# Modulation weights as k-tiles in 8 KB runs, a new order of the first loads, and the context norm between projections

## The chip, the cores and the metric

The kernel runs on one core of a Trainium2 chip. The metric is the device time of one execution in microseconds (us), the median of three runs. The core has five engines that run their own instruction streams and wait for each other on semaphores: TensorE (PE in the profile), VectorE (DVE), ScalarE (ACT), GpSimd (POOL) and SyncE (SP). DMAs are issued by SP, ACT or POOL and carried out by 16 DMA engines.

## The reference, cut to what matters

The reference computes a transformer block with attention and a mixture of experts, and then two more layers of dense mixers. The change lies wholly in the first block, up to its residual sum:

```
mod_l = (silu(c) @ w_ada + b_ada).reshape(6, d)            # c: the condition, d = 1024
mod_c = (silu(c_ctx) @ w_ada + b_ada).reshape(6, d)
sh1, sc1, gt1, sh2, sc2, gt2 = mod_l
hl = rms_norm(x, g_mix) * (1 + sc1) + sh1                  # x: 256 tokens x 1024
pl = hl @ w_in                                             # 1024 x 2048: q, k, v, f
q, k = rope(pl q part), rope(pl k part)
hc = rms_norm(ctx, g_mix) * (1 + csc1) + csh1              # ctx: 256 x 1024
kc, vc = hc @ w_in[:, k and v part]
mix = [diff_attention(q, [kc, k], [vc, v]), fourier_mix(f)]
x = x + gt1 * (mix @ w_out)
h2 = rms_norm(x, g_ffn) * (1 + sc2) + sh2                  # then the experts
```

`w_ada` is 1024 x 6144 in fp32 (24 MB). Its first 2048 columns give sh1 and sc1, which the first projection needs; the other 4096 give gt1, sh2, sc2 and gt2, which are needed only after attention.

## The kernel before

**Tiling.** Weights come in units of 1 MB through a ring of four slots (`ring`). `U_ADA1` are 8 units for sh1 and sc1, `U_IN` 8 units of `w_in`, `U_ADA2` 16 units for the rest of the modulation, `U_OUT` 4 units of `w_out`; then come the experts. A unit of `w_ada`, `w_in` or `w_out` holds all 1024 rows of 256 columns, so its DMA moves 1 KB runs. The experts' units are cut so that a run is 8 KB.

**Order of the loads.** SP issues the units in the order of their numbers. Before each it waits (`vacant`, L532) until the unit four back has been used: `unit_done` for a modulation unit, `w_lo_ready` for a projection's. ACT issues all the rest at its start (L1327 to L1334): the constants' first part, 17 short rows of parameters (among them c, c_ctx and the table of relative positions), x, ctx, the constants' second part, and five side tensors.

**Modulation.** silu(c) and silu(c_ctx) are two columns of a 32 wide stationary tile `csil`. `ada_rows` (L744) takes two units into one PSUM bank of `acc`; four groups of 32 partitions each sum a quarter of the k-tiles. ACT copies the bank out (`mod_row`, L1347), and `ada_cols` (L756) sums the four groups against a selector `sel` and turns the row into columns, four small matmuls for 512 columns. DVE adds the bias (L1844) and makes the scale `a_mix`.

**Before the first projection.** PE waits for the parameter rows, transposes them, takes two pairs of modulation units, transposes x and ctx (L772, L780), and runs the other pairs with the two norms' sums (L722) between them. DVE then scales x by the norm and by 1 + sc1 (L1862), ACT adds the shift and rounds to the high part `h_hi` (L1385), and DVE makes the low part `h_lo` (L1867).

**The projections.** Each fp32 weight unit is split too, by ACT (`split_high`, L497) and DVE (`split_low`, L506), and `project3` runs three matmuls (L669 to L671) in place of an fp32 one. Units 2 to 5 of `w_in` are also used for ctx in plain fp32 (L704, L712). ACT copies each bank out (L1449).

**Attention.** Eight steps s of 128 queries: PE's scores of step s + 1 (L881), then `ada_cols` of the pair before (L761), `ada_rows` of pair 4 + s (L751), the transposes of step s (L890), and after every second step the product with the values (L900). DVE takes maxima (L1895) and combines (L1902 to L1905), ACT exponentiates (L1484). In step 7 ACT has, in this order: the high part of `w_out` unit 0 (`split_high(8)`, issued at the end of step 6), the last `mod_row`, the high part of unit 1 (`split_high(9)`), and the copy of the step's transposes (L1493), for which the last `values` waits.

## Time and profile before

| | us |
|---|---|
| median of 3 runs | 1971.18 |
| lowest and highest | 1965.08 and 1974.21 |
| the profiled execution's own time | 1973.52 |
| its span in the trace | 1971.7 |

The trace's times count from the span's start; some 1.8 us of the profiled execution lie outside the span. The page gives each engine's busy time and the chain of work that ended last. For this change the averages over the span say little: the timelines of the first 215 us, one per engine, say which wait ends last in each stage.

### The profile page before, as it was taken

To read this page: it belongs to the slowest core of one execution; us is meant where nothing else is said; L and a number is where in the kernel's file an instruction comes from. 1 tells how busy PE (TensorE), PEld (TensorE's weight loads), DVE (VectorE), ACT (ScalarE), POOL (GpSimd) and SP (SyncE) were. 2 spreads that over 40 slices of the span, in tenths; PEclk is the share of its full clock that TensorE was granted. 3 is DMA by queue.
4 is the path that set the end of the run, shared out by engine and by line. 5 is a ranking of instruction groups with operands and counts; after the bars stand their busy time and mean duration, and the time that the engine had idled before them with its cause. 6 is when DMAs were issued, how large, how long until landed. Compare 5 with 4: busy or idle time off the path is not lost.

```text
span 1971.7 us, 31086 instructions
## 1 busy us (share of the span) xinstructions
PE 1859.7 (94%) x13331; PEld 1559.5 (79%) x13331; DVE 826.6 (42%) x982; ACT 660.6 (34%) x773; POOL 160.9 (8%) x75
## 2 busy tenths in 40 slices
PE   4898869999999997999999999999999999899998
PEld 2895754445545546999998999999998899899998
DVE  0523531111111117544676554465545345565444
ACT  2514320000000005434435544354344445354433
POOL 0000000000000000111000021112111000111110
PEclk9899969999999998999999999999999999999999
DMA  9336659999999995555534255555554445345550
GB/s 288 123 107 215 216 212 422 421 421 421 422 422 422 422 419 186 180 183 187 177 129 150 98 181 191 174 189 183 182 187 134 150 150 171 129 150 194 192 173 40
DMA packets 224062, 444.26 MB, mean 225 GB/s; under 512 B 11130, under 2 KB 183891, under 8 KB 199259
## 3 DMA queue, kind: packets, MB, share of 16 engines
q1 hardware_dynamic: 217888, 435.74, 60.2%
q10 hardware_dynamic: 6076, 7.08, 1.1%
q8 instruction: 77, 1.26, 0.3%
q14 instruction: 21, 0.17, 0.0%
HBM read 441.73 MB, written 1.06 MB: 225 GB/s over the span
## 4 chain that ended last, share of the span: by engine, by line
PE 88%; DVE 5%; ACT 3%; issue 1%; ACTq 1%; DMA 1%; POOL 0%; DVEq 0%
PE wk L669 13%; PE wk L670 13%; PE wk L671 13%; PE wk L1013 11%; PE acc L669 6%; PE wk L1033 6%; PE acc L671 6%; PE acc L670 6%; PE wk L977 3%; PE acc L993 3%; ACT w_hi L497 1%; PE acc L751 1%; DVE w_lo L506 1%; ACTq L1334 1%; DVE con L2069 1%
## 5 line engine op out<-in xcount | busy, mean ns | idle before, releaser
L506 DVE TENSOR_TENSOR w_lo<-ring,w_hi 128x2048 fp32r<-128x2048 f32 x198 | 452.3, 2287 | 438.4 <-ACT w_hi L497 438.3
L497 ACT ACTIVATE w_hi<-ring 128x2048 fp32r<-128x2048 f32 x199 | 379.4, 1908 | 477.0 <-PE wk L671 319.8
L669 PE MATMUL wk<-h_hi,w_hi 128*128 128x256 f32 x1832 | 524.9, 286 | 14.9 <-DVE h_lo L2058 10.2
L670 PE MATMUL wk<-h_lo,w_hi 128*128 128x256 f32 x1832 | 522.2, 285 | 0.0
L671 PE MATMUL wk<-h_hi,w_lo 128*128 128x256 f32 x1832 | 522.1, 285 | 0.0
L669 PEld LDWEIGHTS wk<-h_hi,w_hi 128*128 128x128 f32 x1832 | 354.7, 194 | 17.9 <-issue 14.4
L670 PEld LDWEIGHTS wk<-h_lo,w_hi 128*128 128x128 f32 x1832 | 354.6, 194 | 0.2
L671 PEld LDWEIGHTS wk<-h_hi,w_lo 128*128 128x128 f32 x1832 | 354.4, 193 | 0.0
L669 PE MATMUL acc<-hid_hi,w_hi 128*128 128x256 f32 x896 | 255.2, 285 | 3.4 <-POOL hid_lo L1766 3.4
L671 PE MATMUL acc<-hid_hi,w_lo 128*128 128x256 f32 x896 | 254.3, 284 | 0.0
L670 PE MATMUL acc<-hid_lo,w_hi 128*128 128x256 f32 x896 | 254.2, 284 | 0.0
L1766 POOL TENSOR_TENSOR hid_lo<-gated,hid_hi 128x512 fp32r<-128x512 f32 x44 | 125.3, 2848 | 1185.8 <-ACT hid_hi L1605 1185.8
L669 PEld LDWEIGHTS acc<-hid_hi,w_hi 128*128 128x128 f32 x896 | 172.2, 192 | 3.6 <-issue 3.6
L670 PEld LDWEIGHTS acc<-hid_lo,w_hi 128*128 128x128 f32 x896 | 172.2, 192 | 0.0
L671 PEld LDWEIGHTS acc<-hid_hi,w_lo 128*128 128x128 f32 x896 | 172.1, 192 | 0.0
L1013 PE MATMUL wk<-ring,arena 128*64 128x512 f32 x512 | 112.6, 592 | 0.8 <-ACT arena L1555 0.8
L1013 PE MATMUL wk<-ex_ring,arena 128*64 128x512 f32 x512 | 112.6, 592 | 0.0
L1555 ACT ACTIVATE arena<-wk 128x512 f32<-128x512 f32 x32 | 19.1, 597 | 267.5 <-PE wk L977 267.5
L669 PE MATMUL wk<-w_hi,h_hi 128*128 128x256 f32 (+1 forms) x336 | 99.9, 297 | 2.9 <-DVE h_lo L2058 2.9
L2022 DVE SCALAR_TENSOR_TENSOR arena<-wk,slot_gate,arena 128x512 f32<-128x512 f32 x16 | 12.0, 751 | 209.2 <-PE wk L1013 209.2
L670 PE MATMUL wk<-w_lo,h_hi 128*128 128x256 f32 (+1 forms) x336 | 96.0, 286 | 0.0
L671 PE MATMUL wk<-w_hi,h_lo 128*128 128x256 f32 (+1 forms) x336 | 96.0, 286 | 0.0
(299 smaller groups left out, 1991.5 us busy)
## 6 DMA issues: line engine op xcount, KB each, us to landing
ring<-in_ffn_w_in_dram SPq DMA_DIRECT2D x88, 1024.0 KB, 5.0
ring<-in_w_gate_dram SPq DMA_DIRECT2D x64, 1024.0 KB, 13.8
ex_ring<-in_w_up_dram SPq DMA_DIRECT2D x64, 1024.0 KB, 17.1
ring<-in_ffn_w_out_dram SPq DMA_DIRECT2D x44, 1024.0 KB, 4.8
ex_ring<-in_w_down_dram SPq DMA_DIRECT2D x32, 1024.0 KB, 13.6
arena<-in_w_down_dram SPq DMA_DIRECT2D x32, 1024.0 KB, 12.7
ring<-in_w_ada_dram SPq DMA_DIRECT2D x24, 1024.0 KB, 8.8
ring<-in_b_w_in_dram SPq DMA_DIRECT2D x24, 1024.0 KB, 5.2
```

What stands on the lines that cost most here:

```text
L497: nc.scalar.activation(w_hi[:, v % SPLIT, 0:n], ring[:, u % RING, 0:n], ACT.Copy).then_inc(w_hi_ready, 1)
L506: eng.tensor_tensor(w_lo[:, v % SPLIT, 0:n], ring[:, u % RING, 0:n], w_hi[:, v % SPLIT, 0:n].bitcast(F32), ALU.subtract).then_inc(w_lo_rea ...
L669: mm(dst, w[0], x[0], start=first, stop=False, skip_group_check=True)
L670: mm(dst, w[0], x[1], start=False, stop=False, skip_group_check=True)
L671: return mm(dst, w[1], x[0], start=False, stop=last, skip_group_check=True)
L751: last = mm(accf[lane:lane + 32, bank * 512 + j * UW:bank * 512 + (j + 1) * UW], csil[:, k, :], slot_cols(u)[:, k, :], start=(k < ADA_GROU ...
L977: last = mm(wk[:, 1, q * P:(q + 1) * P], h2[:, t, 4 * half + q, :], pick_at[:, t, :], start=(t == 0), stop=(t == TT - 1))
L993: last = mm(acc[:, m, :], y_rows[:, m * P:(m + 1) * P], spread[:, p % 2, :], start=(p == 0 and m % 2 == 0), stop=True, skip_group_check=True)
L1013: last = mm(wk[own, s // 2, :], xg[:, p % 2, k, own], ex_slot(2 * s + j)[:, q * DE:(q + 1) * DE], start=(k == 0), stop=(k == KT - 1), skip ...
L1033: last = mm(wk[own, 2 + half, :], hidT[:, 2 * s + f, own], ex_slot(8 + 2 * s + j)[:, c:c + 512], start=(s == 0 and f == 0), stop=(s == 1 a ...
L1334: act.dma_start(dst, src).then_inc(side_in, 16)
L1766: nc.gpsimd.tensor_tensor(dst, src, hi.bitcast(F32), ALU.subtract).then_inc(ready, 1)
```

## The change

- **Loads of the modulation.** `ada_v` is cut by k-tile: a unit is 128 rows of 2048 columns, so a run is 8 KB, and eight units make one group of 2048 columns. Units stay 1 MB, and there are still 8 and 16.
- **Modulation on PE.** A unit is four matmuls with 512 columns instead of eight with 256; they accumulate over eight units in one bank. Each of the four partition groups now holds other columns, so `sel` gets 8 columns and `ada_cols` runs once for 2048 columns, with the same four matmuls: three times in all instead of twelve.
- **Order of the loads.** x goes first on SP's queue, then the eight units, two units of `w_in`, ctx, and the rest. On ACT's queue c and c_ctx come right after the constants' first part, which shrinks (642 to 264 columns). The second part and the side tensors (cut in two where they are the router's) are issued by POOL after the first projection's unit is done.
- **Order on PE.** c is transposed first, then x, then the modulation units in the order of arrival with the parameter rows' transposes and x's norm among them. The first projection unit starts in halves. The transposes of ctx come after it, the norm of ctx and the matmul for lambda after the second unit, the table of relative positions after the fourth. The ctx projections of units 2 and 3 come after both units' three-piece ones.
- **x's chain.** DVE multiplies x by the inverse root (one instruction) before the modulation is there. Then ACT makes `h_hi` with scale and shift in one step, and DVE the unrounded value (`shifted`) and the low part.
- **Attention.** The transposes of all steps use one PSUM bank, `ada_cols` runs before step 4's units and at the end.

```diff
+            sp.dma_start(x_rows, x[0].rearrange("(t p) d -> p t d", p=P)).then_inc(x_in, 16)
             for a in range(8):
-                fetch(U_ADA1 + a, slot_cols(U_ADA1 + a), ada_v[a])
-            for a in range(8):
+                fetch(U_ADA1 + a, ring[:, (U_ADA1 + a) % RING, :], ada_v[0, a])
+            for a in range(2):
+                fetch(U_IN + a, slot_cols(U_IN + a), in_v[a])
+            sp.dma_start(c_rows, ctx[0].rearrange("(t p) d -> p t d", p=P)).then_inc(ctx_in, 16)
+            for a in range(2, 8):
                 fetch(U_IN + a, slot_cols(U_IN + a), in_v[a])
...
+            def ada_rows(u, k, bank):
+
+                arrived(u)
+                for gr in range(ADA_GROUPS):
+                    last = mm(accf[32 * gr:32 * gr + 32, bank * 512:(bank + 1) * 512], csil[:, k, :],
+                              ring[:, u % RING, gr * 512:(gr + 1) * 512], start=(k == 0), stop=(k == KT - 1),
+                              skip_group_check=True)
+                last.then_inc(unit_done, 1)
...
+            def first_unit(b):
+
+                pe.wait_ge(first_lo, 1)
+                project3(b, 0, fresh=0, ks=range(KT // 2), closes=False)
+                split(U_IN)
+                return project3(b, 0, fresh=0, ks=range(KT // 2, KT), opens=False)
+
+            pe.wait_ge(std_ready, 1)
+            group(first_unit, ends_unit=True)
+            pe.wait_ge(ctx_in, 16)
+            pe.wait_ge(mod_ready, 1)
+            for t in range(TT):
+                for k in range(KT):
+                    last = nc.tensor.transpose(acc[:, k, t * P:(t + 1) * P], c_rows[:, t, k * P:(k + 1) * P], ident)
+            last.then_inc(ctx_ps, 1)
+            v = split(U_IN + 1)
+            group(lambda b: project3(b, v), ends_unit=True)
+            norm(1, 0, accf[:, 0:T])
...
+            for a in range(2, 4):
                 v = split(U_IN + a)
-                group(lambda b: project3(b, v, fresh=None if a else 0), ends_unit=True)
-            pe.wait_ge(lame_ready, 1)
+                group(lambda b: project3(b, v))
+            pe.wait_ge(tables_in, 16)
+            mm(accf[0:HEADS2, 512:1024], reltab[:, :], buckets[0:32, :], start=True, stop=True).then_inc(rel_ps, 1)
+            pe.wait_ge(h_shifted, 1)
...
-                if s:
-                    ada_cols(3 + s)
-                    pe.wait_ge(at_ready, s)
-                ada_rows(4 + s, (s + 1) % 2)
+                if s == 4:
+                    ada_cols(1)
+                for a in (2 * s, 2 * s + 1):
+                    ada_rows(U_ADA2 + a, a % KT, 1)
                 turn(s)
...
-            act.dma_start(con[:, FIRST:], consts[:, FIRST:]).then_inc(tables_in, 16)
-            for dst, src in SIDE:
-                act.dma_start(dst, src).then_inc(side_in, 16)
...
+            def scaled_high(k):
+
+                A(h_hi[:, k, :], hT[:, k, :], ACT.Identity, bias=mod[:, k, 0:1],
+                  scale=a_mix[:, 0, k:k + 1]).then_inc(h_hi_ready, 1)
...
+            pool.wait_ge(unit_done, U_IN + 1)
+            pool.dma_start(con[:, FIRST:], consts[:, FIRST:]).then_inc(tables_in, 16)
+            for dst, src in SIDE:
+                pool.dma_start(dst, src).then_inc(side_in, 16)
...
+            def shifted(k):
+
+                return V.tensor_scalar(hcT[:, k, :], hT[:, k, :], a_mix[:, 0, k:k + 1], mod[:, k, 0:1], ALU.mult, ALU.add)
```

PE, from its start to the first projection, before (L740 to L743 the parameter rows, L751 modulation, L772 x, L780 ctx, L761 the turn into columns, L722 the norms):

```order
L740 MATMUL wk<-con,scr 128x128
L741 MATMUL wk<-con,scr 128x89
L742 MATMUL wk<-con,scr 64x4
L743 MATMUL wk<-con,reltab 8x512
L751 MATMUL acc<-ring,gated 32x256 x32
L772 MATMUL acc<-con,arena 128x128 x16
L780 MATMUL wk<-con,arena 128x128 x16
L751 MATMUL acc<-ring,gated 32x256 x16
L761 MATMUL acc<-con,gated 128x2 x8
L722 MATMUL wk<-scr,con 128x256 x8
L751 MATMUL acc<-ring,gated 32x256 x16
L722 MATMUL wk<-scr,con 128x256 x8
```

The same stretch of PE now (L770 is c, L774 x, L754 modulation, L780 to L782 the parameter rows, L734 x's norm, L764 the columns, L680 the first projection):

```order
L770 MATMUL acc<-con,scr 128x16
L774 MATMUL wk<-con,arena 128x128 x16
L754 MATMUL acc<-ring,gated 32x512 x8
L780 MATMUL acc<-con,scr 128x128
L781 MATMUL acc<-con,scr 128x73
L782 MATMUL acc<-con,scr 64x4
L754 MATMUL acc<-ring,gated 32x512 x8
L734 MATMUL wk<-scr,con 128x256 x8
L754 MATMUL acc<-ring,gated 32x512 x16
L764 MATMUL acc<-con,gated 128x8 x4
L680 MATMUL wk<-h_hi,w_hi 128x256
```

What is gone from this stretch is the table of relative positions, the transposes of ctx, one norm and three of four turns into columns; a modulation matmul is twice as wide and there are half as many.

ACT before, its last DMA issues and what follows:

```order
L1329 DMA scr<-in_rel_table_dram 32x8
L1330 DMA arena<-in_x_dram 128x2x1024
L1331 DMA arena<-in_ctx_dram 128x2x1024
L1332 DMA con<-in_consts_dram 128x2888
L1334 DMA arena<-in_w_fourier_dram 128x4x128
L1334 DMA arena<-in_w_router_group_dram 128x8x4
L1334 DMA arena<-in_w_router_expert_dram 128x8x32
L1334 DMA arena<-in_b_router_group_dram 1x4
L1334 DMA arena<-in_b_router_expert_dram 1x32
L1337 ACT_TABLE_LOAD
L1337 ACTIVATE cols<-wk 128x128
```

ACT now, from the same place (L1347 is the silu, L1349 to L1351 the parameter columns, L1363 x's squares, L1358 the copy of the modulation rows):

```order
L1344 DMA reltab<-in_rel_table_dram 32x8
L1347 ACT_TABLE_LOAD
L1347 ACTIVATE gated<-acc 128x8x2
L1349 ACTIVATE cols<-acc 128x128
L1350 ACTIVATE cols<-acc 128x73
L1351 ACTIVATE cols<-acc 64x4
L1363 ACTIVATE scr<-xT 128x512 x4
L1369 ACT_TABLE_LOAD
L1369 ACTIVATE std<-wk,small 128x256
L1358 ACTIVATE gated<-acc 128x512
```

Eight issues are gone from between the parameter rows and ACT's first activation.

PE in attention, steps 1 and 2 before (L881 scores, L761 columns, L751 modulation, L890 transposes):

```order
L881 MATMUL wk<-arena 128x512 x2
L761 MATMUL acc<-con,gated 128x2 x4
L751 MATMUL acc<-ring,gated 32x256 x16
L890 MATMUL acc<-con,arena 128x128 x4
L881 MATMUL wk<-arena 128x512 x2
L761 MATMUL acc<-con,gated 128x2 x4
L751 MATMUL acc<-ring,gated 32x256 x16
L890 MATMUL acc<-con,arena 128x128 x4
```

and now:

```order
L894 MATMUL wk<-arena 128x512 x2
L754 MATMUL acc<-ring,gated 32x512 x8
L903 MATMUL acc<-con,arena 128x128 x4
L894 MATMUL wk<-arena 128x512 x2
L754 MATMUL acc<-ring,gated 32x512 x8
L903 MATMUL acc<-con,arena 128x128 x4
```

The turn into columns is gone from between the scores and the modulation units.

## Rows read from the trace of the kernel before

**Rows 1.** The page, busy time of each engine and its share of the span.
```profile
PE 1859.7 (94%) x13331; PEld 1559.5 (79%) x13331; DVE 826.6 (42%) x982; ACT 660.6 (34%) x773; POOL 160.9 (8%) x75
```
**Rows 2.** Windows by stage: length, busy time per engine, PE's clock, DMA share, GB/s.
```profile
0.00:63.20 63.20, 27.46 (x231) 18.65 (x231) 12.81 (x24) 20.89 (x33) 0.20 (x4) 0.97 0.89 285
63.20:139.60 76.40, 76.35 (x511) 73.05 (x512) 22.93 (x24) 22.30 (x28) 3.13 (x2) 0.96 0.31 98
160.70:214.00 53.30, 43.95 (x405) 26.38 (x403) 25.76 (x53) 26.10 (x55) 0.36 (x1) 0.92 0.97 309
```
**Rows 3.** Timeline of 0:32: start us, us, engine, line, instruction.
```profile
7.57 0.32 ACTq L1329 DMA_DIRECT2D reltab<-in_rel_table_dram  x1
11.41 10.72 ACTq L1334 DMA_DIRECT2D arena<-in_w_router_expert_dram  x1
12.64 0.45 PE L740 MATMUL wk<-con,scr 128*128 128x128 f32 x1 [12.64 <-DMA reltab<-in_rel_table_dram]
26.32 1.28 ACT L1337 ACT_TABLE_LOAD   x1 [26.32 <-issue]
30.12 6.20 PE L751 MATMUL acc<-ring,gated 128*32 128x256 f32 x64 [14.94 <-ACT gated L1343]
```
**Rows 4.** Pieces of the chain that ended last, 30:64: start us, us, what.
```profile
37.13 1.95 PE acc L772 x16
...
43.39 1.88 PE acc L761 x16
...
50.69 3.67 PE wk L722 x16
...
58.98 0.18 DVE small L1844 x2
...
59.46 3.26 DVE scr L1862 x8
62.71 0.41 DVE h_lo L1867
...
63.25 0.55 PE wk L669
```
**Rows 5.** Windows, columns as in rows 2: 1 KB runs from SP, then the experts' 8 KB.
```profile
0.00:10.00 10.00, 0.00 (x0) 0.00 (x0) 0.37 (x3) 0.00 (x0) 0.20 (x4) 1.00 0.86 244
...
180.00:200.00 20.00, 18.59 (x192) 11.36 (x184) 9.77 (x24) 10.16 (x24) 0.00 (x0) 1.00 1.09 349
...
400.00:700.00 300.00, 300.00 (x1574) 147.56 (x1572) 37.37 (x121) 23.88 (x40) 0.00 (x0) 1.00 1.01 422
```
**Rows 6.** Timeline: single instructions that price an operation of the change.
```profile
13.31 1.87 PE L743 MATMUL wk<-con,reltab 32*8 32x512 f32 x2
...
163.29 0.49 DVE L1904 TENSOR_SCALAR arena<-arena,small 128x512 f32<-128x512 f32 x1
...
228.48 1.22 DVE L1926 TENSOR_TENSOR h_lo<-arena,h_hi 128x1024 fp32r<-128x1024 f32 x1 [1.13 <-ACT h_hi L1531]
```
**Rows 7.** Windows, columns as in rows 2: the first 6 us of the projections.
```profile
63.20:69.40 6.20, 6.15 (x29) 6.18 (x30) 6.20 (x16) 4.68 (x11) 0.00 (x0) 0.50 0.05 18
```
**Rows 8.** Timeline of attention, 160:218: DVE's end of two steps, PE, then ACT.
```profile
176.32 0.75 DVE L1905 SCALAR_TENSOR_TENSOR arena<-arena,small 128x512 f32<-128x512 f32 x1
...
181.14 0.75 DVE L1905 SCALAR_TENSOR_TENSOR arena<-arena,small 128x512 f32<-128x512 f32 x1
...
167.34 1.86 PE L761 MATMUL acc<-con,gated 128*128 128x2 f32 x8
...
205.07 1.07 PE L751 MATMUL acc<-ring,gated 128*32 128x256 f32 x16 [1.84 <-DMA ring<-in_w_ada_dram]
...
213.96 3.75 PE L900 MATMUL acc<-arena 128*128 128x256 f32 x8 [2.33 <-ACT arena L1499]
...
208.12 1.91 ACT L497 ACTIVATE w_hi<-ring 128x2048 fp32r<-128x2048 f32 x1 [6.19 <-DMA ring<-in_w_out_dram]
...
211.14 1.91 ACT L497 ACTIVATE w_hi<-ring 128x2048 fp32r<-128x2048 f32 x1 [0.63 <-DMA ring<-in_w_out_dram]
```

285 lines of the change are left out of this document (146 added, 139 removed).

## The prediction

> **What bounds the kernel now.** I read the page first. PE is busy for 94% of the span [rows 1], which looks as if loads at the start could not matter. But the average covers stages with different limits, and the change touches only the first 214 us. The windows by stage [rows 2] divide them: up to 63.2 us PE works 27.46 us of 63.20; from there to 139.6 it works without a gap (76.35 of 76.40); in attention, 160.7 to 214.0, the DMAs are busy for 0.97 of the time. So the start and attention can give something, and in the projections every microsecond of PE work added is a microsecond lost.
>
> In the start, the timeline shows two waits. PE could begin at 12.64 us, when the last parameter row has landed, but ACT is still issuing DMAs: one of the router's takes 10.72 us of its queue, and ACT's first activation starts at 26.32. Since silu(c) comes after it, the first modulation matmul starts at 30.12 [rows 3], when four units have long been in the ring and no further one could be fetched. From there to 63.25 the chain is PE work of x, ctx, two norms and the modulation, then DVE and ACT [rows 4].
>
> In attention the chain passes through DMAs. ACT's high part of the first `w_out` unit waits 6.19 us for its DMA until 208.12, that of the second until 211.14, and behind both stands the copy for which the last product with the values (213.96) waits [rows 8]. At 1 KB runs the queue moves 349 GB/s; in the experts, at 8 KB, it moves 422 [rows 5].
>
> **The start.** With ACT's queue ending at the parameter rows (7.57 + 0.32), the silu is ready near 9.5 us, and x, now first on SP's queue, near 6. From then on the modulation is bound by its DMAs: each slot is freed by a unit's matmuls, some 1.6 us [rows 3], less than a unit's transfer. What must have landed is x and eight units, 9.4 MB, and 0.2 MB of small things. I take for the first 10 us what it moved before, 244 GB/s or 2.4 MB, and for the other 7.2 MB the 422 GB/s of 8 KB runs [rows 5]: 17.0 us. The last unit is there at 27.0. At the 349 GB/s of 1 KB runs it would be 30.6; these are the two ends of this term, and I take the first because the row with the same run length and the same SP queue is the nearest.
>
> Behind it lies a chain: the last unit's matmuls 1.7 us (64 records, four units' worth, took 6.20, a part of it at the lower clock; so 1.55 for one unit, and a little more if all of it is at the lower clock) [rows 3]; ACT's copy 0.6; four small matmuls 1.0 at the upper clock (16 records took 1.88 [rows 4]) and 1.9 at the lower [rows 8], I take 1.4; the bias and scale on DVE 0.5 to 1.2 (58.98 to 59.46, and what lies before), I take 1.0. That makes 31.7. DVE then computes eight unrounded tiles. The tensor-scalar of 512 columns took 0.49 [rows 6]; with some 0.2 of it fixed, one of 256 costs 0.27 in a row, 2.2 in all; the upper bound is the 3.26 of L1862 [rows 4]. A half of `w_lo` is 1.22 [rows 6], the first `h_lo` 0.41 [rows 4], hand-overs 0.4: the first three-piece matmul starts at 36.0, in place of 63.25. ACT's `h_hi` and the first `w_in` unit (3.0 us behind the last modulation unit, 30.0, and its half high part 31.0) come earlier than that and cost nothing; if that cover goes, a late `w_in` unit costs its lateness. **Term: -27.2 us**, with ends of -30 (short DVE steps, PE at full clock) and -22.5 (1 KB rate and the slow DVE row).
>
> **The projections.** Their own work stays, 76.4 us, with the same slow beginning at half clock [rows 7]. What moves in between them is on PE, with nothing to hide it: ctx's transposes 1.9 (16 records, as x's in 1.95), one norm 1.9 (half of 3.67) [rows 4], the sum for lambda 0.3, and the table of relative positions 1.2 to 1.9 (1.87 at 13.31 [rows 6]). **Term: +5.4 us.** Waits that could be added: ctx has landed by 38, before the first unit ends (44). The second norm's squares end near 50.5, while PE is in unit 2 until 51.6. The matmul of relative positions waits for POOL's DMA of 1.7 MB, issued at 44 and wanted at 65; behind that wait PE's remaining projections are queued. `h_shifted` is there near 60. I cost these at nothing, by 1 to 20 us of cover.
>
> Here the Trainium skill speaks against the change: its page "SBUF — State Buffer", § SBUF: two separate sides, says that a DMA issued by POOL gets its descriptors from GpSimd, which cannot write them while VectorE holds the shared port. No run here shows a DMA from POOL. By that rule the tables would come late by part of DVE's busy time in that stretch; the cover of 21 us would have to be used up before it costs.
>
> **Attention.** Ten modulation units are moved in the saturated part, now in 1.049 MB / 422 GB/s = 2.49 us instead of 3.00: 5.1 us. It also begins earlier: the columns' 1.86 us before step 1's units, at the lower clock [rows 8], are gone. That gives 1.9 us more for the first `w_out` unit, 201 instead of 208.1. But then the steps themselves are as long: one without a DMA wait takes 181.14 - 176.32 = 4.82 us from combine to combine, where two units take 4.98, and three of the eight also hold a product with the values, at full clock half of 3.75 [rows 8]. This chain ends within 2 us of the DMA. **Term: -7.0 us**, ends -2 (units no faster, only the start earlier) and -8.5 (the 1.84 us wait at 205.07 gone as well).
>
> **What follows.** The experts' loads wait for free slots, not for a time, so that nothing there absorbs the shift: their stage is bound at 422 GB/s [rows 5] from when it begins, and it begins later than its slots are filled. The code from there is the same.
>
> **Sum.** 1973.5 of the profiled execution - 27.2 + 5.4 - 7.0 = 1944.7. That execution is 2.3 us over the median, so against the median 1942.4; I say 1942.
>
> **Rivals.**
> 1. *8 KB runs of w_ada move no faster than 1 KB runs.* For it: rows of `w_ada` lie 24 KB apart, while an expert's tile is read in one piece, so the 422 may belong to the layout. Against it: 349 is also the rate of every 1 KB load I looked at. Then the start gives 23.6 instead of 27.2 and attention 2 to 3: 1942 + 3.6 + 4.5 = 1950, with a late `w_in` 1952. The skill's page "DMA: Bandwidth & Descriptors", § Where 436 GB/s comes from, would have it so: it says that for loads from HBM the memory side, about 358 GB/s for a core, is the limit. By that rule, the trace disagrees: 422 over 300 us. Chance 0.12.
> 2. *A hand-over comes late.* The short rows (512 B) share the DMA engines with packets of 4 and 8 KB. If the parameter rows land not at 12.6 but at 22, PE's wait for them stands in front of the third unit, no slot is freed, and the queue runs dry for some 5 us. The same price has a stall of ctx's squares or of the tables. 1947 to 1952. Chance 0.13.
> 3. *More is gained*: the start at 33 and attention -8.5, 1936. Chance 0.08.
> 4. *The gain is given back*: some wait later is tied to the DMAs' progress and not to PE's. I found none; 1966 to 1976. Chance 0.03.
> 5. *Slower.* The tables and side tensors through POOL. PE's queue stands behind the tables' landing in the middle of the projections. It costs only when they land after 65 us, and turns the gain of 29 into a loss when they land after 94, 50 us from their issue. The nearest row is ACT's 10.72 us for one router tensor [rows 3]; at that price for each of eight transfers, and with the tables served last, they land at 44 + 86 = 130, 65 us late, and the kernel takes 1942 + 65 = 2007. It needs that order or that price for the tables alone; issued first, they are more likely near one such price, 55 us, inside the cover. Chance 0.02.
>
> **How the numbers follow.** The forecast has 0.62, its own range 1937 to 1947. The range that should hold the time 8 times in 10 leaves out rivals 4 and 5 and about half of what is over 1950 and under 1936: 1934 to 1953. A measurement of this kernel tells 0.5%, some 10 us, from no change; so all under 1961 is faster: 0.62 + 0.12 + 0.13 + 0.08 = 0.95, and I give 0.94. Same 0.04, slower 0.02.
>
> **What would show it.** Right: ACT's first activation before 10 us; the eight modulation units' matmuls one every 2.5 us, the last near 27; the first three-piece matmul at 34 to 38; PE without gaps until about 117; over 400 GB/s in attention; the `w_out` wait ending near 179 (201 - 22). Wrong: modulation matmuls 3 us apart (rival 1), a gap of PE before the parameter rows' transposes or before ctx's norm (rival 2), PE waiting for a DMA issued by POOL (rival 5), or an end of the first block that moves less than the first projection does.

## The result, and the profile after

The changed kernel takes **1945.72 us** (median of four runs, 1943.99 to 1947.01), beside 1972.36 for the kernel before, measured with it: ratio 0.9872, 95% interval 0.9849 to 0.9895. It is 26.6 us faster; forecast were 29, with the time at 1942. In the measurements of the experiments the kernel before had medians of 1969.5 to 1970.5, so the difference is good to some 2 us. The profiled execution took 1944.74 us, its span is 1943.0.

Windows by stage (length, busy time per engine in the order PE, PEld, DVE, ACT, POOL, then PE's clock, DMA share, GB/s), to set against [rows 2, 5]:

```profile
0.00:10.00 10.00, 2.75 (x13) 2.75 (x14) 0.36 (x3) 1.47 (x2) 0.20 (x4) 1.00 0.81 301
10.00:20.00 10.00, 5.06 (x33) 1.79 (x35) 2.58 (x4) 0.95 (x5) 0.00 (x0) 0.94 1.02 416
20.00:30.00 10.00, 9.45 (x64) 3.99 (x52) 3.31 (x2) 3.32 (x6) 0.00 (x0) 0.89 0.85 292
30.00:37.20 7.20, 1.50 (x14) 0.97 (x8) 5.58 (x16) 3.82 (x7) 0.00 (x0) 0.67 1.08 378
37.20:120.20 83.00, 82.95 (x548) 77.96 (x549) 24.77 (x26) 31.75 (x43) 8.57 (x10) 0.97 0.45 153
141.20:189.30 48.10, 35.21 (x229) 15.74 (x227) 25.94 (x55) 22.73 (x49) 0.33 (x1) 0.97 0.95 348
```

The start is 26 us shorter. The projections are still all PE (82.95 of 83.00) but take 83.0 us where they took 76.5. In the start the rate is 416 GB/s while modulation units come in. In attention it is 348 on average: 415 at 150 to 160, less where the DMAs have nothing to fetch, and the `w_out` units at its end move in 1 KB runs.

The start on PE (timeline: start us, us, engine, line, instruction; the bracket is idle time ahead and what ended it), to set against [rows 3, 4]. L770 is c, L774 x, L754 modulation, L780 the parameter rows, L734 x's norm, L764 the columns, L680 the first three-piece matmul:

```profile
7.25 0.26 PE L770 MATMUL acc<-con,scr 16*128 16x16 f32 x1 [7.25 <-DMA scr<-in_c_ctx_dram]
7.43 3.67 PE L774 MATMUL wk<-con,arena 128*128 128x128 f32 x16
11.04 2.49 PE L754 MATMUL acc<-ring,gated 128*32 128x512 f32 x16
18.47 0.33 PE L780 MATMUL acc<-con,scr 128*128 128x128 f32 x1 [4.94 <-DMA reltab<-in_rel_table_dram]
...
22.39 3.72 PE L734 MATMUL wk<-scr,con 128*128 128x256 f32 x16
26.05 2.78 PE L754 MATMUL acc<-ring,gated 128*32 128x512 f32 x24
29.37 1.06 PE L754 MATMUL acc<-ring,gated 128*32 128x512 f32 x8 [0.55 <-DMA ring<-in_w_ada_dram]
31.16 1.06 PE L764 MATMUL acc<-con,gated 128*128 128x8 f32 x8 [0.72 <-ACT gated L1358]
37.25 0.55 PE L680 MATMUL wk<-h_hi,w_hi 128*128 128x256 f32 x1 [5.04 <-DVE h_lo L1892]
```

The first modulation matmul comes at 11.04 in place of 30.12, the first three-piece one at 37.25 in place of 63.25. One wait stands where the forecast had none: 4.94 us for the parameter rows, whose last landed at 18.47, 10.9 us after its issue at 7.57. While PE stood there no slot was freed, and the 292 GB/s at 20 to 30 us show the hole that this left (391 in the same ten microseconds of the kernel with late rows, below).

What was put between the projections, from the chain of work that ended last (start us, us, what): ctx's transposes, its norm, lambda, the table of relative positions.

```profile
45.63 1.75 PE acc L814 x16
...
53.13 3.45 PE acc L734 x16
56.58 0.31 PE acc L820 x2
...
68.60 0.95 PE acc L825 x2
```

POOL's DMA issues in the same stretch; no instruction of PE waits for what they load. The constants' second part landed 9.5 us after its issue, and PE wanted it at 68.5:

```profile
45.95 0.73 POOL L1797 DMA_DIRECT2D con<-in_consts_dram  x1 [45.42 <-PE wk L682]
46.67 0.80 POOL L1799 DMA_DIRECT2D arena<-in_w_fourier_dram  x1
56.59 0.77 POOL L1799 DMA_DIRECT2D arena<-in_w_router_group_dram  x1 [9.12 <-issue]
```

The end of attention, to set against [rows 8], PE and then ACT. L903 are the transposes of the last step, L913 products with the values, L504 high parts of `w_out`, L1504 the copy of the transposes:

```profile
179.92 0.66 PE L903 MATMUL acc<-con,arena 128*128 128x128 f32 x4
180.41 1.89 PE L913 MATMUL acc<-arena 128*128 128x256 f32 x8
185.92 1.77 PE L764 MATMUL acc<-con,gated 128*128 128x8 f32 x8 [2.76 <-ACT gated L1358]
189.30 3.73 PE L913 MATMUL acc<-arena 128*128 128x256 f32 x8 [1.60 <-ACT arena L1510]
...
183.47 1.91 ACT L504 ACTIVATE w_hi<-ring 128x2048 fp32r<-128x2048 f32 x1 [4.71 <-DMA ring<-in_w_out_dram]
185.29 0.58 ACT L1358 ACTIVATE gated<-acc 128x512 f32<-128x512 f32 x1
186.49 1.91 ACT L504 ACTIVATE w_hi<-ring 128x2048 fp32r<-128x2048 f32 x1 [0.62 <-DMA ring<-in_w_out_dram]
188.30 0.58 ACT L1504 ACTIVATE arena<-acc 128x512 f32<-128x512 f32 x1
```

The wait for `w_out` ends last again. All times that the experiments are compared by, from PE's timelines (us; the rope matmuls end the projections; "values" is the last product with the values, "router" the router's first matmul):

| kernel | first three-piece | to rope | first scores | to values | router | time |
|---|---|---|---|---|---|---|
| before | 63.25 | 76.5 | 158.78 | 55.2 | 254.1 | 1972.4 |
| changed | 37.25 | 83.0 | 139.25 | 50.1 | 228.6 | 1945.7 |
| short runs | 40.49 | 82.6 | 142.07 | 51.9 | 236.9 | 1952.2 |
| rows late | 35.06 | 82.8 | 136.88 | 48.2 | 225.1 | 1943.9 |
| tables on ACT | 48.30 | 82.1 | 149.44 | 50.1 | 239.8 | 1955.6 (one run) |
| side tensors by POOL, in before | 57.33 | 76.1 | 152.47 | 52.0 | 247.5 | 1963.3 |
| quarter units | 36.82 | 83.2 | 139.01 | 48.6 | 231.2 | 1948.1 (one run) |
| columns each step | 37.84 | 82.0 | 138.91 | 49.5 | 227.4 | 1948.4 (one run) |
| tail order | 37.88 | 81.9 | 138.77 | 44.6 | 229.3 | 1947.5 |
| tail order, filler | 38.04 | 82.2 | 139.22 | 44.6 | 228.0 | 1947.7 |
| rows late, filler | 35.36 | 80.9 | 135.29 | 50.0 | 224.9 | 1943.1 |
| ctx early | 38.44 | 75.4 | 132.84 | 50.3 | 222.6 | 1941.1 |
| ctx early, halves | 37.64 | 76.7 | 133.33 | 50.0 | 222.6 | 1941.3 |
| ctx early, split norm | 40.51 | 77.9 | 137.42 | 50.8 | 228.0 | 1942.8 |

The quarter units leave out three quarters of the later modulation, so only the stretch up to the router is read there. The intervals of the ratios to the kernel before are given where one decides.

### The profile page after: what moved, and what is told of

It reads as the page before. It is cut to its first block, busy times and chain, and to the rows that moved or that the text cites. A ratio compares the mean times of both kernels' runs of the same rounds, so it can differ in the third digit from the quotient of the medians.

```text
span 1943.0 us, 30548 instructions
## 1 busy us (share of the span) xinstructions
PE 1845.9 (95%) x13068; PEld 1542.4 (79%) x13068; DVE 828.1 (43%) x986; ACT 655.1 (34%) x767; POOL 166.9 (9%) x83
## 3 DMA queue, kind: packets, MB, share of 16 engines
HBM read 441.73 MB, written 1.06 MB: 228 GB/s over the span
## 4 chain that ended last, share of the span: by engine, by line
PE 88%; DVE 6%; ACT 3%; DMA 1%; issue 1%; ACTq 0%; POOL 0%; DVEq 0%
PE wk L680 13%; PE wk L681 13%; PE wk L682 13%; PE wk L1026 11%; PE wk L1046 6%; PE acc L680 6%; PE acc L682 6%; PE acc L681 6%; PE wk L990 3%; PE acc L1006 3%; ACT w_hi L504 1%; DVE con L2112 1%; DVE w_lo L513 1%; PE wk L1258 1%; PE wk L715 1%
## 5 line engine op out<-in xcount | busy, mean ns | idle before, releaser
L680 PE MATMUL wk<-h_hi,w_hi 128*128 128x256 f32 x1832 | 526.3, 287 | 14.5 <-DVE h_lo L2101 9.5
L504 ACT ACTIVATE w_hi<-ring 128x2048 fp32r<-128x2048 f32 x198 | 377.4, 1907 | 481.0 <-PE wk L682 324.7
L680 PEld LDWEIGHTS wk<-h_hi,w_hi 128*128 128x128 f32 x1832 | 357.2, 195 | 17.5 <-issue 14.7
L680 PE MATMUL acc<-hid_hi,w_hi 128*128 128x256 f32 x896 | 254.5, 284 | 3.2 <-POOL hid_lo L1779 3.2
L680 PEld LDWEIGHTS acc<-hid_hi,w_hi 128*128 128x128 f32 x896 | 171.9, 192 | 3.3 <-issue 3.3
L680 PE MATMUL wk<-w_hi,h_hi 128*128 128x256 f32 (+1 forms) x336 | 98.4, 293 | 3.0 <-DVE h_lo L2101 3.0
L1026 PEld LDWEIGHTS wk<-ring,arena 128*64 128x64 f32 x512 | 37.1, 137 | 73.0 <-issue 72.2
```

Source lines behind the costliest of these rows:

```text
L504: nc.scalar.activation(w_hi[:, v % SPLIT, 0:n], ring[:, u % RING, 0:n], ACT.Copy).then_inc(w_hi_ready, 1)
L680: mm(dst, w[0], x[0], start=first, stop=False, skip_group_check=True)
L1026: last = mm(wk[own, s // 2, :], xg[:, p % 2, k, own], ex_slot(2 * s + j)[:, q * DE:(q + 1) * DE], start=(k == 0), stop=(k == KT - 1), skip ...
```

## The experiments

**Run length.** Each modulation unit of the changed kernel as two DMAs of 1 KB runs:

```diff
+                dst = ring[:, u % RING, :].rearrange("p (i j f) -> p j i f", j=2, f=UW)
+                src = src.rearrange("p (i j f) -> p j i f", j=2, f=UW)
+                sp.dma_start(dst[:, 0], src[:, 0]).then_inc(odd_in[u % RING], 16)
+                sp.dma_start(dst[:, 1], src[:, 1]).then_inc(weights_in[u % RING], 16)
...
-                fetch(U_ADA1 + a, ring[:, (U_ADA1 + a) % RING, :], ada_v[0, a])
+                fetch_short(U_ADA1 + a, ada_v[0, a])
```

> The kernel after, with every modulation unit moved in 1 KB runs: two DMAs for a unit, one for the even and one for the odd 256-column pieces; bytes, order and everything else as after. Theory (the run length sets the rate): about 350 GB/s in attention in place of over 400, the last modulation unit of the start 1 to 3 us later, the first three-piece matmul at 38 to 41 in place of 37.25, and from the first scores to the last product with the values 53 to 55 us in place of 50.05; in all 5 to 9 us slower than after. Rival (the rate belongs to something else, the layout or the queue): both as after within 1 us. The same run tells why the parameter rows land at 18.5: if they share the DMA engines packet by packet with 4 and 8 KB packets, they land by 14 here; if it is the number of bytes ahead of them, they stay at 18 or later.

1952.22, ratio 0.9911 (0.9887 to 0.9934), +6.5 us. PE's timeline of that kernel (here L764 is modulation, L790 the rows), and its window of 10 to 20 us:

```profile
14.03 0.33 PE L790 MATMUL acc<-con,scr 128*128 128x128 f32 x1
...
16.03 1.06 PE L764 MATMUL acc<-ring,gated 128*32 128x512 f32 x8 [1.48 <-DMA ring<-in_w_ada_dram]
19.06 1.93 PE L764 MATMUL acc<-ring,gated 128*32 128x512 f32 x8 [1.96 <-DMA ring<-in_w_ada_dram]
```
```profile
10.00:20.00 10.00, 5.37 (x39) 1.43 (x38) 2.58 (x4) 3.80 (x8) 0.00 (x0) 0.88 1.10 347
```

A unit every 3.03 us, 347 GB/s for 416. The edit also makes two DMAs of each unit, but the kernel before moved 1 KB runs in one DMA per unit at 349 GB/s [rows 5], so it is the run length that sets the rate, and the prediction's first rival is out. Of the 8.3 us at the router, run length explains 2.8 (first scores) and 1.9 (attention); the other 3.7 come behind attention, mostly from a collision of DVE and POOL that is shown with the tail's experiments. And PE does not wait for the rows, which have landed by 14.03 instead of 18.47: short rows on ACT's queue are held up by long runs on SP's. That agrees with the Trainium skill, "DMA: Bandwidth & Descriptors", § Queues, rings and completion order, which says that a DMA engine serves its queues in turn and drains a whole packet of several descriptors from one before it switches.

**Rows late.** The parameter rows get a place of their own, and PE takes them after x's norm:

```diff
-            pe.wait_ge(rows_in, 16 * N_ROWS)
-            nc.tensor.transpose(accf[:, 16:16 + P], rows1, ident)
...
             for a in range(2, 4):
                 ada_rows(U_ADA1 + a, a, 3)
             pe.wait_ge(x_ready, 1)
             norm(0, 0)
+            pe.wait_ge(rows_in, 16 * N_ROWS)
+            nc.tensor.transpose(accf[:, 16:16 + P], rows1, ident)
...
```

ACT's copies of these rows and what DVE computes from them move behind the norm too, so ACT's squares of x no longer stand behind the wait.

> The kernel after, with the parameter rows in a place of their own and their transposes and copies moved behind x's norm, so that PE doesn't wait for them before the third modulation unit. Theory (the late rows hold back the slots, and so the loads): the third unit's matmuls start near 14 in place of 18.94, the last unit lands near 27 in place of 29.4, the first three-piece matmul starts near 35 in place of 37.25; 2 us off the time. Rival (the loads are bound by bytes and start-up alone, PE's wait is hidden): the last unit still lands at 29 or later and nothing is gained.

The last modulation unit comes at 27.16, a unit every 2.5 us, and the first three-piece matmul at 35.06, 2.2 us earlier; the whole 1943.87 (ratio 0.9879, 0.9856 to 0.9902), and the router 3.5 us earlier. The theory holds in the trace; in the medians the difference to the changed kernel, 1.9 us, is inside their spread.

**ACT's queue.** The tables and side tensors of the changed kernel back on ACT, behind the rows; and, the other way round, the side tensors of the kernel before issued by POOL:

```diff
+            act.dma_start(con[:, FIRST:], consts[:, FIRST:]).then_inc(tables_in, 16)
+            for dst, src in SIDE:
+                act.dma_start(dst, src).then_inc(side_in, 16)
...
-            pool.wait_ge(unit_done, U_IN + 1)
-            pool.dma_start(con[:, FIRST:], consts[:, FIRST:]).then_inc(tables_in, 16)
-            for dst, src in SIDE:
-                pool.dma_start(dst, src).then_inc(side_in, 16)
```

> The kernel after, with one part undone: the constants' second part and the side tensors (the router's still cut in two) are issued by ACT behind the parameter rows, as before, not by POOL. Theory (ACT's queue blocks): ACT's first activation at 20 to 27 in place of 9.27, the first three-piece matmul at 48 to 54. Rival (cut in two they don't block the queue; only their 1.9 MB share the DMAs): first activation by 12, first three-piece matmul at 40 to 43.

> The kernel before, with one part of the change alone: the side tensors (router and Fourier weights, router biases) are issued by POOL after the first projection unit, not by ACT before its first activation. Theory (most of the start's gain is that ACT's queue no longer blocks the silu): the first modulation matmul at 17 to 18 in place of 30.12, the first three-piece matmul near 51 in place of 63.25, nothing else moves; 12 us faster than before. Rival (the loads bind the start anyway): the first three-piece matmul at 56 or later.

ACT's timeline with the tables on ACT:

```profile
8.55 8.08 ACTq L1347 DMA_DIRECT2D arena<-in_w_router_group_dram  x2
16.65 4.30 ACTq L1347 DMA_DIRECT2D arena<-in_w_router_expert_dram  x2
...
21.88 1.28 ACT L1350 ACT_TABLE_LOAD   x1 [21.88 <-issue]
```

Halved, the router's tensors still take 12.4 us of the queue; the first three-piece matmul comes 11 us later, as the theory has it, and the whole is at 1955.6. In the kernel before, freeing the queue moves the first modulation matmul from 30.12 to 18.15 and the first three-piece one by only 5.9 us (1963.26, ratio 0.9971, 0.9957 to 0.9984), since then PE waits for units; that is the rival's case, not the theory's:

```profile
18.15 4.36 PE L753 MATMUL acc<-ring,gated 128*32 128x256 f32 x48 [2.54 <-ACT gated L1342]
26.25 1.93 PE L753 MATMUL acc<-ring,gated 128*32 128x256 f32 x16 [3.74 <-DMA ring<-in_w_ada_dram]
```

So in the kernel before the queue alone is worth 6 of the start's 26 us, and in the changed one, where the loads come faster, 11; the rest needs the order of the loads, the run length and the shorter chain with it.

**Attention: what bounds it now.** Two changes to the changed kernel, one that takes load off the DMAs and one that puts the columns back:

```diff
-                fetch(U_ADA2 + a, ring[:, (U_ADA2 + a) % RING, :], ada_v[1 + a // KT, a % KT])
+                fetch(U_ADA2 + a, ring[:, (U_ADA2 + a) % RING, 0:512], ada_v[1 + a // KT, a % KT][:, 0:512])
```
```diff
                 if s == 4:
                     ada_cols(1)
+                elif s:
+                    for m in range(4):
+                        mm(accf[:, 1216 + 8 * m:1224 + 8 * m], ones, sel, start=True, stop=True)
```

> The changed kernel, in which each of the sixteen later modulation units loads only the first 512 of its 2048 columns, 2 KB runs and a quarter of the bytes. The rest of the slot keeps what was there, so three quarters of gt1, sh2, sc2 and gt2 are left out and the routing after attention may differ: only the stretch before the router is read. In the changed kernel the first scores start at 139.25, the last product with the values at 189.30, 50.05 us later. Theory A (the eight steps are bound by the chain PE, DVE, ACT, 4.82 us a step, and only the tail behind the last step by the loads of w_out): the steps stay at 4.82, the last combine stays 39.0 us behind the first scores, the first w_out unit no longer keeps ACT waiting, its high part starts near 178.8 and the last product with the values near 184.7, 45.4 us behind the first scores. Theory B (the loads bind the steps too): the steps fall under 4.82 and the last product comes at 178 or earlier, under 39 us. Theory C (the tail is not bound by loads either): 189, 50 us.

> The changed kernel with four more small matmuls between scores and modulation units in steps 1 to 3 and 5 to 7, where the kernel before turned its pair of units into columns; their result is not used. What the removed turns into columns were worth in attention: theory A (PE is idle 1.25 us in each step, waiting for DVE's combine, so 1.06 us of small matmuls fit in): the steps stay at 4.82 us, the slots come free about 1 us later, and the last product with the values starts 0 to 1.2 us later, 50.1 to 51.3 us behind the first scores. Theory B (they lengthen the steps): six times 1.06, 56.4 us.

In the changed kernel DVE's combines stand 4.81, 4.83, 4.82, 6.55, 4.83, 6.55 us apart (6.55 where a product with the values lies between). With a quarter of the bytes they stand as far apart, but for one step in which PE's clock was low (0.81 at 141 to 150): the steps are not bound by loads. The tail is only in part: ACT still waits for `w_out`, until 181.75,

```profile
181.75 1.91 ACT L504 ACTIVATE w_hi<-ring 128x2048 fp32r<-128x2048 f32 x1 [2.04 <-DMA ring<-in_w_out_dram]
```

5.4 us after the issue at 176.37, in place of 8.05 after 175.42. The load is issued when step 6 frees a slot, so it comes at the steps' pace, not at the DMAs'. Theory A had the mechanism right and expected 3.2 us too much of it (48.6 us to the values, not 45.4), 1.2 of which are the slow step. With the columns back attention is no longer (49.5), Theory A: in the steps without a product PE idles 1.25 us, which is room for 1.06 us of small matmuls. (The router comes at 231.2 in the first of these, later than in the changed kernel; the next section tells why.)

A slow step is also in the profiled execution of the kernel before, and a larger one. Its step 1 took 7.7 us. The kernel before with the side tensors by POOL runs the same instructions in attention, and its step 1 took 4.8. The windows of that step, first the kernel before, then the other:

```profile
164.60:172.30 7.70, 7.68 (x48) 4.06 (x48) 2.86 (x6) 2.13 (x6) 0.00 (x0) 0.56 0.66 217
```
```profile
158.30:163.10 4.80, 4.56 (x48) 2.62 (x48) 2.85 (x6) 2.25 (x7) 0.00 (x0) 1.00 1.00 331
```

PE's granted clock was 0.56 in one and 1.00 in the other. So 2.9 of the 5.1 us by which attention got shorter from the first row of the table to the second are the clock of one execution and not the change. Against the other kernel's 52.0 us the change gives 2. The changed kernel with short runs, which does without the columns of each step too, takes 51.9, so these 2 us are the run length's. That is as much as the stretch differs between executions (48.2 to 50.8 in those with 8 KB runs and the tail unchanged), so the size is rough.

**The tail's order on ACT.** The copy of step 7's transposes goes ahead of the high parts of `w_out`; then the same with eight unread matmuls in PE's idle time:

```diff
-                if s == 7:
-                    split_high(9)
                 turned(s)
-                if s == 6:
-                    split_high(8)
...
+            split_high(8)
             head_root(0)
+            split_high(9)
             head_out(3)
```
```diff
+            for _ in range(8):
+                mm(wk[:, 3, 0:2 * P], ones, con[:, 0:2 * P], start=True, stop=True)
             pe.wait_ge(mix_lo_ready, 2)
```

> The changed kernel with one other order on ACT behind the last attention step: the copy of step 7's transposes and head 2's output go ahead of the high part of the first w_out unit, and the sub-norm's first root ahead of that of the second. Nothing is left out. Theory A (the last product with the values waited at 189.30 only since ACT, in its own order, waited for the w_out loads until 183.47 and 186.49): the product starts near 182 to 183, and since DVE's two splits, two reciprocals and the low part stand behind 185.4 anyway (14.9 us in a row, end near 200.5 to 201.5 where it now is 204.1), the router's matmul comes 3 us earlier (225.5 in place of 228.6) and the kernel takes 1942.7. Theory B (the w_out loads bind it anyway): the product early, the router's matmul within 1 us of 228.6, 1945.

> The changed kernel with ACT's other order at the end of attention (1947.5 us, router's matmul 229.3 although the last product with the values was 6 us earlier), and eight matmuls of 256 columns, read by nobody, where PE then stood idle for 4.07 us before the second part of the output projection. Theory A (in that run the gain of the tail was eaten by the clock: PE's granted clock fell to 0.58 at 204 to 208 after the 4 us of idling): the second part starts near 203.5 at full clock, the router's matmul comes 2 to 3.3 us earlier, 226 to 227.3, 1944.5 in all. Theory B (the clock there is not the cause): router's matmul 229, 1947.

The last product with the values comes at 183.32, 6 us earlier, and nothing is left of it at the router: Theory B's numbers, but not for its reason. Timelines of the first of the two, PE, POOL, then DVE:

```profile
203.45 0.39 PE L680 MATMUL acc<-h_hi,w_hi 128*128 128x256 f32 x1 [4.07 <-DVE h_lo L1967]
...
191.60 4.59 POOL L513 TENSOR_TENSOR w_lo<-ring,w_hi 128x2048 fp32r<-128x2048 f32 x1 [50.55 <-ACT w_hi L504]
...
194.34 2.52 DVE L1962 SCALAR_TENSOR_TENSOR arena<-arena,small,gated 128x256 f32<-128x256 f32 x2
```

DVE's chain of splits, reciprocals and scalings ends at 203.4 where it ended at 204.1, so PE only waits longer, 4.07 us. Part of that chain got slower: the two scalings took 2.52 us, and 0.88 in the changed kernel. They began while POOL computed a `w_lo` (191.60 to 196.19) and were done at 196.86, behind it. In the changed kernel they had ended 0.6 us before POOL began:

```profile
194.58 0.88 DVE L1964 SCALAR_TENSOR_TENSOR arena<-arena,small,gated 128x256 f32<-128x256 f32 x2
```
```profile
196.06 4.58 POOL L513 TENSOR_TENSOR w_lo<-ring,w_hi 128x2048 fp32r<-128x2048 f32 x1 [54.54 <-ACT w_hi L504]
```

With quarter units the same pair, begun 0.3 us after POOL, took 4.98 us (the pair also met POOL with short runs, 5.22, and with the side tensors by POOL, 5.24):

```profile
192.56 4.58 POOL L513 TENSOR_TENSOR w_lo<-ring,w_hi 128x2048 fp32r<-128x2048 f32 x1 [51.28 <-ACT w_hi L504]
...
192.84 4.98 DVE L1964 SCALAR_TENSOR_TENSOR arena<-arena,small,gated 128x256 f32<-128x256 f32 x2
```

The Trainium skill, "SBUF — State Buffer", § SBUF: two separate sides, has such a rule (a DVE operation with two SBUF inputs and a GpSimd one that reads SBUF exclude each other for a whole instruction), and these rows agree with it. The other part is PE's clock: after its 4 us of idling the granted clock was 0.66 and 0.50 in the two windows from 204 to 208; with the filler it was 1.00 in both, and the router came 1.4 us earlier, in an execution whose first scores came 0.5 us later. The time did not follow (1947.7). So the tail's wait for `w_out`, though it ends last in attention, was worth nothing by itself: DVE's chain is as late.

**ctx's place.** Late rows, and ctx back ahead of the first projection, with its norm where PE waits for DVE and ACT. Then late rows alone with six unread matmuls in that gap. The diff is of the first, against the changed kernel, without the part that moves the rows:

```diff
+                if a == 3:
+                    sp.dma_start(c_rows, ctx[0].rearrange("(t p) d -> p t d", p=P)).then_inc(ctx_in, 16)
...
-            for a in range(2, 4):
+            for a in range(4, 6):
                 ada_rows(U_ADA1 + a, a, 3)
...
-            for a in range(4, 8):
+            pe.wait_ge(ctx_in, 16)
+            for t in range(TT):
+                for k in range(KT):
+                    last = nc.tensor.transpose(wkf[:, k, t * P:(t + 1) * P], c_rows[:, t, k * P:(k + 1) * P], ident)
+            last.then_inc(ctx_ps, 1)
+            for a in range(6, 8):
                 ada_rows(U_ADA1 + a, a, 3)
             ada_cols(0)
+            norm(1, 0, accf[:, 3 * T:4 * T])
```

ACT copies and squares ctx before it copies the modulation rows.

> The changed kernel with the parameter rows late (as in the run of that name: 1943.9 us, first three-piece matmul near 35, first scores at 136.9) and with ctx where the kernel before had it, ahead of the first projection: its load stands behind the fourth modulation unit on SP's queue, PE transposes it after the sixth unit and sums its norm while DVE and ACT prepare the first projection, with squares in the buffer of x's rows. Theory A (the move between the projections takes 1.75 + 3.45 us of PE out of its idle time and puts them on the path; loading ctx earlier costs 1.05 MB / 0.42 = 2.5 us of the queue): the first three-piece matmul starts near 37.5, projections take 77.9 us from there to the rope matmuls instead of 83.1, the first scores come near 134.3, the whole is 2.7 us faster than with late rows alone, 1941.2. Theory B (the move was right because ctx's load and its work between the units cost the start more than that): first three-piece at 40 or later, first scores 137 or later, 1944 or more.

> The kernel with late parameter rows, and after the columns of the first modulation six matmuls of 256 columns whose result nobody reads, in the 5 us in which PE waits for DVE and ACT to prepare the first projection. What it tells: with ctx early (norm in that gap) the projections took 75.37 us, 7.6 less than with ctx between them, where the moved work is only 1.75 + 3.45; the granted clock over the first 6 us was 1.00 instead of 0.54. Theory A (the gap makes the projections start at half clock, and that costs 2.4 us): the fillers run at 29.9 to 34.5, the first three-piece matmul stays at 35.1, the clock of the next 6 us is 0.9 to 1.0, first three-piece to rope 80.4 in place of 82.8, first scores 134.5, the whole 2 to 2.5 us faster than with late rows alone. Theory B (the clock there does not bind, since PE waits for splits by DVE and ACT anyway): 82.8 as before, scores at 136.9, same time.

ctx early takes 1941.14 (1938.94 to 1943.73; ratio 0.9859, 0.9842 to 0.9875), and its windows at the beginning of the projections and PE's norm read (the third fence is the same first 6 us in the changed kernel):

```profile
38.40:44.40 6.00, 6.00 (x52) 5.99 (x51) 6.00 (x10) 4.68 (x5) 0.00 (x0) 1.00 0.87 273
```
```profile
33.25 5.39 PE L736 MATMUL acc<-arena,con 128*128 128x256 f32 x16
```
```profile
37.20:43.20 6.00, 5.95 (x30) 5.98 (x31) 4.84 (x9) 5.09 (x7) 0.00 (x0) 0.54 1.09 350
```

The first three-piece matmul comes 3.4 us later than with late rows alone, the projections are 7.4 us shorter, the first scores come 4.0 us earlier, and the router 2.5: the first step of attention ran at a low clock again (0.71, 5.66 us for 4.81). That is Theory A, with the time at its 1941.2. Against the changed kernel the traces show 6 us at the router, while the intervals of the two ratios overlap. Of the 7.4 us by which the projections are shorter, only 5.2 are the moved work (1.75 + 3.45). The rest is the clock: PE worked up to the start of the projections and had the upper level (2.4 GHz) from the first matmul, where after 5 us of idling it had the lower one (0.54 of full speed on average). The filler shows that alone: projections 80.9 for 82.8 us. But there the first step of attention took 5.61 us for 4.81 and the `w_out` load landed as late as before, so the router gained 0.1 us and the time (1943.1) cannot be told from that of late rows.

**Two attempts to go further.** DVE's preparation in halves together with ctx's norm in two pieces, then the split norm alone. The cuts are against ctx early; both kernels also transpose ctx one modulation unit earlier:

```diff
-            for k in range(KT):
+            for k in range(KT // 2):
                 last = shifted(k)
             link(last)
...
+            for k in range(KT // 2, KT):
+                last = shifted(k)
+            link(last)
             dve.wait_ge(w_hi_ready, 1)
```
```diff
+            norm(1, 0, accf[:, 3 * T:4 * T], range(KT // 2))
             ada_rows(U_ADA1 + 7, 7, 3)
             ada_cols(0)
-            norm(1, 0, accf[:, 3 * T:4 * T])
+            norm(1, 0, accf[:, 3 * T:4 * T], range(KT // 2, KT))
```

> Late rows and early ctx as before, ctx's transposes one unit earlier, its norm in two halves (one before the last modulation unit, one behind the columns), and DVE computes the unrounded x in two halves, with the first half of w_lo between them. Nothing is left out. Theory A (in the run with ctx early PE's norm until 38.6 and DVE's low part at 38.3 bound the first three-piece matmul together, so both have to be shortened): DVE's first w_lo half starts when ACT has w_hi (34.6), the first low part is there at 36.3 to 37.0, PE's second half norm ends at 35.3, first three-piece at 36.6 to 37.1 in place of 38.44, clock still high, first scores 131.3 to 131.6, the whole 1.2 to 1.9 us faster than with ctx early: 1939.3 to 1940. Theory B (the added idle time brings the half clock back, or the second half of w_lo comes late): first scores at 132.8 or later, 1941 or more.

> The kernel with ctx early, ctx's transposes one unit earlier and its norm in two halves, as in the run before, but with DVE's order as in the changed kernel: all eight unrounded tiles, then the first half of w_lo. In the run before, the first three-piece matmul came 0.8 us earlier (37.64 for 38.44) but the first scores 0.5 us later (133.33 for 132.84): PE then waited 0.80 us for the second half's low part. Theory A (DVE's work in halves is at fault, since the second half stands behind more of it than PE's first half covers): first three-piece at 38.2 to 38.5, no wait in the first unit, first to rope 75.4, first scores 132.6 to 132.9, 1941. Theory B (the split norm is at fault, through the 1.9 us of idle PE that it leaves ahead of the projections): projections 76.5 or more, first scores 133.3 or later.

1941.33 and 1942.77: neither gains on ctx early. With the halves PE starts 0.8 us earlier and then waits 0.80 us for the second half. In the last run neither theory's numbers came: the first half of the norm took 3.68 us (and 1.99 in the run before, with the same instructions ahead of it on PE), which made the last modulation unit 1.6 us late; the granted clock at 28 to 32 us was 0.64, and 1.00 in the run before. Which of the two parts costs is left open; that PE's clock in the start differs from execution to execution is what the pair shows.

## Why the prediction was right, step by step

**Start, -27.2 forecast, -26.0 measured.** The mechanism held: ACT's first activation at 9.27, the modulation bound by its loads at 8 KB rate, the chain behind the last unit. Two sizes were off, in opposite senses. The last unit's matmuls came at 29.37, not 27.0: that is the second rival's case, "parameter rows late", which I had put at 22 us and 5 us of dry queue; it was 18.5 and cost 2.2 (late rows: 27.16). In return the chain from there to the first three-piece matmul took 7.9 us, where I had summed 9.0, mostly since PE's four small matmuls and the unit ran at full clock (1.06 each, for 1.4 and 1.7); the eight unrounded tiles took 2.67 for 2.2. That late rows alone hit the forecast's 27.0 (27.16) is partly luck: the first 10 us moved 301 GB/s and not 244 (by my estimate from these rates 1.4 us), and the sum had nothing for the time between a unit's last byte and PE's start on it.

**Projections, +5.4 forecast, +6.5 measured.** The path was right, PE with nothing to hide behind. The mis-sized term is the norm: I took "half of 3.67" for one norm from [rows 4], but that row's 16 records are one norm (eight fp32 matmuls, two records each), and it costs 3.45. Transposes (1.75), lambda (0.31) and the table (0.95) were near or under their estimates; 1.75 + 3.45 + 0.31 + 0.95 = 6.46. That the first 6 us stay at half clock was right, but I had counted it as a constant; it was a cost that the change could have removed, 1.9 us by the filler (with the rows late).

**Attention, -7.0 forecast, -5.1 measured, of which the change made about 2.** I priced ten units at 0.51 us each and the earlier start at 1.9, as if the stretch stayed bound by loads. It does not: with 8 KB runs the DMAs stand idle in part (317 GB/s at 160 to 170), and the steps run at their own 4.82 and 6.55 us. What the run length took away are the waits for units late in attention (0.88 and 1.84 us before); what stands last now is the `w_out` load, which is issued when step 6 frees a slot. I had named that chain ("ends within 2 us of the DMA") and should have summed it instead. The columns' 1.86 us [rows 8] lay in the one step that ran at half clock, and I took them for a cost that the change removes; put back, they cost nothing measurable, and another execution of the same instructions had no slow step. So this term came near by luck: 2.9 us of it are that step.

**After attention** I had said that nothing changes, and the shift at the router is 25.6 us for 24.7 at the last product with the values. It is not a fixed stretch, though: with ACT's order unchanged it took 39.0 to 40.3 us where DVE's scalings miss POOL's `w_lo`, and 42.9 to 43.6 where they meet it.

**The sum.** By the traces' terms it is -26.0 + 6.5 - 5.1 - 0.9 = -25.5, against 26.6 between the medians. The forecast for the profiled execution, 1944.7, met 1944.74, and that is luck: its terms were 4.2 us too large together, and the two profiled executions differ by another 3.1 us behind the router, where the code is the same (that stretch took 1714 to 1719 us in all traces).

**The signs.** Of those that I had named as right, ACT's early start (its table load at 7.98, the activation at 9.27), the first three-piece matmul (37.25) and the gapless projections came, the last until 120.2 and not 117. The `w_out` wait ended at 183.47 and not near 179, and 415 GB/s in attention held for a part of it only. Two signs of being wrong came as well: PE's gap before the parameter rows (rival 2), and an end of the first block that moved by less (25.6 at the router, 24.7 at the values) than the first projection (26.0). The second tells that the whole gain is the start's: from the first three-piece matmul to the router the kernel before took 190.9 us and the changed one 191.3, since the moved work on PE (6.5) outweighs what attention gave.

**The rivals.** The first (8 KB runs no faster) is refuted by the short runs. Its rule, that the memory side limits loads at about 358 GB/s, stands in the Trainium skill, "DMA: Bandwidth & Descriptors", § Where 436 GB/s comes from; the trace has 416 for rows that lie 24 KB apart. The second came true at less than half its price. The fifth (tables late by POOL) did not come near: POOL's issues stood up to 9 us apart, as the quoted rows show, but PE never waited for them, and moved back to ACT they cost 10 us. Whether DVE held POOL up there, by the rule that the prediction cites, is not shown: DVE worked for only 2.3 of the 9.1 us of the longest gap. What was missing from the list is that the change could have been better placed: ctx ahead of the projection, its norm in time that PE spends idle anyway.

## What to carry to other kernels

Before moving work out of a start-up phase, look for the idle time that remains in it afterwards: the 5 us in which PE waits for the splits of the first operand held a whole norm (until 38.6, where DVE's first low part came at 38.3), and work there also kept PE's clock up for what followed. A wait that "ends last" is worth its length only if the next engine's chain behind it is not as late; sum that chain from its busy times before pricing the wait. Count records per operation before taking a duration from a grouped row. Before pricing a row that was taken at a low clock as a cost of the code, look whether another execution has the same clock there.

## What the runs showed of the hardware

- Short rows issued on ACT's queue landed 10.9 us after their issue beside 8 KB runs on SP's queue, and over 4 us earlier beside 1 KB runs.
- Transfers of 1 MB to 128 partitions went at 416 GB/s with 8 KB runs and at 347 with 1 KB runs, in the same stretch of otherwise equal kernels.
- Two DVE scalings of 256 columns with two tensor inputs took 0.88 us, and 2.52, 4.98, 5.22 or 5.24 when they met a 4.6 us elementwise operation of POOL; DVE's reciprocals beside POOL kept their 3.35 us.
- After PE had idled for 5.04 us (ahead of the projections) the granted clock was 0.54 over the next 6 us (0.58 with the rows late), and after 4.07 us (tail's order) 0.66 and 0.50 in the next two windows of 2 us; with unread matmuls in the same gaps it was 0.91 and 1.00.
- In two executions with the same instructions on PE up to that point, the same eight records of a norm took 1.99 and 3.68 us, by the clock granted there (1.00 and 0.64). In two others one step of attention, with the same instructions, took 4.8 us at 1.00 and 7.7 at 0.56.
